# The exponent's argument in the mLSTM chunks: four operations with two sources and a per-partition scalar, one for each head, in place of a sum and a minimum over all heads

## The reference, cut to what matters

```python
D = bcum[..., :, None] - bcum[..., None, :] + ib[..., None, :]
D = jnp.where(mask, D, -jnp.inf)
g = bcum + m[..., None]
m_t = jnp.maximum(g, jnp.max(D, axis=-1))
inter = jnp.exp(g - m_t)
S = jnp.einsum('bhtd,bhsd->bhts', qb, kb) * jnp.exp(D - m_t[..., None])
num = jnp.einsum('bhts,bhsd->bhtd', S, vb) + inter[..., None] * jnp.einsum('bhvk,bhtk->bhtv', C, qb)
...
C_new = decay[..., None, None] * C + jnp.einsum('bhs,bhsv,bhsk->bhvk', w, vb, kb)
```

## Time and profile before

| What | us |
|---|---|
| median of 3 runs | 1199.9 |
| lowest and highest | 1199.41, 1201.68 |
| the profiled execution, own time | 1196.64 |
| its span, first to last instruction | 1194.9 |
| PE busy | 1144.2 (96%) |
| DVE busy | 706.8 (59%) |
| ACT busy | 428.1 (36%) |
| POOL busy | 305.2 (26%) |

### The profile page before, as it was taken

One profiled execution on the slowest core, in us unless ns is written; L12 is line 12 of the kernel. 1 busy time (PEld: TensorE's weight loads), 2 busy tenths in 40 slices (PEclk: granted clock), 3 DMA queues, 4 the chain that ended last, 5 costly groups with the idle time before them and its releaser, 6 DMA issues.

```text
span 1194.9 us, 19527 instructions
## 1 busy us (share of the span) xinstructions
PE 1144.2 (96%) x7381; PEld 1095.4 (92%) x7381; DVE 706.8 (59%) x1253; ACT 428.1 (36%) x716; POOL 305.2 (26%) x263
## 2 busy tenths in 40 slices
PE   5899999999989999999999999999999999999997
PEld 2698888888878999899999999999999999999996
DVE  4561455587876434787656655655645745656746
ACT  5552355545455343641320421321411311412331
POOL 0441101110535366771210210210210210210252
PEclk9999999999999999999999999999999999999998
DMA  8813334666343722120121121120120111111104
GB/s 305 312 62 111 108 107 141 202 191 203 105 135 118 245 72 71 37 71 27 45 71 36 37 71 36 53 70 18 53 70 18 70 53 31 56 53 36 36 1 142
DMA packets 61702, 109.87 MB, mean 92 GB/s; under 512 B 6434, under 2 KB 30278, under 8 KB 61254
## 3 DMA queue, kind: packets, MB, share of 16 engines
q1 hardware_dynamic: 51430, 84.88, 21.4%
q10 hardware_dynamic: 10208, 24.12, 6.5%
HBM read 96.81 MB, written 12.18 MB: 91 GB/s over the span
## 4 chain that ended last, share of the span: by engine, by line
PE 65%; DVE 3%; ACT 2%; issue 1%; POOL 0%; POOLq 0%; ACTq 0%; DVEq 0%
PE D L2297 13%; PE D L2299 13%; PE D L2298 13%; PE X L2299 5%; PE X L2297 5%; PE X L2298 5%; PE D L2113 3%; PE D L2115 3%; PE D L2114 3%; POOL H_lo L975 0%; DVE X L1556 0%; DVE B L1542 0%; ACT L1207 0%; DVE FU L1684 0%; DVE FU L1750 0%
## 5 line engine op out<-in xcount | busy, mean ns | idle before, releaser
L975 POOL TENSOR_TENSOR Y_lo<-FU,Y_hi 128x344 fp32r<-128x344 f32 (+2 forms) x120 | 123.1, 1030 | 555.3 <-ACT Y_hi L1115 548.9
L1831 DVE SCALAR_TENSOR_TENSOR X<-D,MOD,X 128x344 f32<-128x344 f32 (+1 forms) x216 | 123.8, 573 | 136.4 <-PE D L2299 113.9
L2297 PE MATMUL D<-Y_hi,W_hi 128*128 128x344 f32 x576 | 185.0, 321 | 0.0
L2298 PE MATMUL D<-Y_lo,W_hi 128*128 128x344 f32 x576 | 183.9, 319 | 0.0
L2299 PE MATMUL D<-Y_hi,W_lo 128*128 128x344 f32 x576 | 183.9, 319 | 0.0
L2113 PE MATMUL D<-H_hi,W_hi 128*128 128x344 f32 x472 | 157.7, 334 | 3.7 <-POOL H_lo L975 3.1
L2115 PE MATMUL D<-H_hi,W_lo 128*128 128x344 f32 x472 | 151.5, 321 | 0.0
L2114 PE MATMUL D<-H_lo,W_hi 128*128 128x344 f32 x472 | 151.5, 321 | 0.0
L2297 PEld LDWEIGHTS D<-Y_hi,W_hi 128*128 128x128 f32 x576 | 108.4, 188 | 1.2 <-issue 0.9
L2299 PEld LDWEIGHTS D<-Y_hi,W_lo 128*128 128x128 f32 x576 | 108.3, 188 | 0.0
L970 POOL TENSOR_TENSOR W_lo<-RAWW,W_hi 128x1024 fp32r<-128x1024 f32 x25 | 61.4, 2457 | 183.6 <-ACT W_hi L1110 183.1
(11 more groups left out here) (358 smaller groups left out, 2658.7 us busy)
## 6 DMA issues: line engine op xcount, KB each, us to landing
RAWW<-in_W SPq DMA_DIRECT2D x76, 512.0 KB, 3.6
RAWW<-in_WADA ACTq DMA_DIRECT2D x28, 512.0 KB, 4.3
RAWW<-in_WADA SPq DMA_DIRECT2D x20, 512.0 KB, 8.0
RAWW<-in_W ACTq DMA_DIRECT2D x18, 512.0 KB, 4.2
X0T<-in_x SPq DMA_DIRECT2D x3, 1376.0 KB, 12.6
out_y<-OUTN SPq DMA_DIRECT2D x24, 172.0 KB
X<-in_x SPq DMA_DIRECT2D x8, 344.0 KB, 4.4
NM<-nm_d SPq DMA_DIRECT2D x8, 256.0 KB, 6.0
```

Of the source, the lines that this page charges most:

```text
L975: nc.gpsimd.tensor_tensor(lo_v, fu_v, hi_v.bitcast(F32), ALU.subtract).then_inc(lo_ready, 1)
L1831: tell(V.scalar_tensor_tensor(out=tile(X, m_x, a, a + w), in0=DB[bank][:, 0:w], scalar=tile(MOD, m_g, 0, 1), in1=tile(X, m_x, a, a + w), o ...
L2297: T.matmul(out, w_h, hi(kt), start=(kt == 0), stop=False)
L2298: T.matmul(out, w_h, lo(kt), start=False, stop=False)
```

## The change

The two operations over 4 heads x 128 columns become four operations of 128 columns, each on one head: (`NM` + the head's column of `COL`) min `MASK`. Each of the first three is followed by a wait for itself (`link`), the last raises `ex_ready` as before. Nothing else is changed; the order of the steps is the same.

```diff
                     dve.wait_ge(ld_nm, 16 * (c + 1))
-                    link(V.tensor_tensor(EX[:], NM[:], wide(colh(0, c), LC), ALU.add))
-                    tell(V.tensor_tensor(EX[:], EX[:], over(MASK[:], HEADS), ALU.min), ex_ready, c + 1)
+                    for h in range(HEADS):
+                        one = V.scalar_tensor_tensor(out=EX[:, h, :], in0=NM[:, h, :], scalar=colh(0, c)[:, h:h + 1], in1=MASK[:],
+                                                     op0=ALU.add, op1=ALU.min)
+                        if h < HEADS - 1:
+                            link(one)
+                    tell(one, ex_ready, c + 1)
```

## The result

The change made the kernel **slower by 0.28%**: 1203.91 us median of 19 runs (1200.54 to 1206.23) against 1200.12 of 19 runs before (1196.86 to 1202.92), ratio 1.0028 with a 95% interval of 1.0020 to 1.0036, so 3.4 us with 2.4 to 4.3. The forecast was 1200.6, no measurable change, range 1198.6 to 1202.6. Two repeats gave 1.0013 (0.9998 to 1.0029) and 1.0019 (1.0008 to 1.0030). So the three series put the loss at 1.6 to 3.4 us; the interval of one of them still reaches no change.

What follows compares the result with a forecast made beforehand. PE was taken to lead the mixing stage, its waits mostly ending with DVE. Chunk delays of 0.09 + 0.27 + 0.3 = 0.7 us, put on the median 1199.9, gave 1200.6 us, range 1198.6 to 1202.6.

Steps and rivals of the forecast that it cites:

- The price of the added operations: DVE's `EX` step: 0.351 us per operation, 0.385 from start to start, 1.54 against 1.45 us, so 0.09 longer a chunk.
- The rival of the cheap operation: Each new DVE operation costs only 0.29 us, each step is 0.15 us shorter, 1199.15 us in all; chance 0.03.
- What of it reaches the end: Mixing stage, chunk by chunk: how much of DVE's longer step delays the end through PE's waits; 0.7 us in all.
- Chunks 0 to 4: Delay reaching the end: nothing in chunks 0 and 2, 0.09 (perhaps 0.2) us in 1, 0.09 each in 3 and 4.
- one of the two cases given: Chunk 1, L1722 before the change: POOL starts a little later, or one more short DVE instruction is left behind it.
- Chunk 6: POOL's L975 falls within the step, which ends at 328.7 to 328.85 instead of 328.50; 0.3 us reaches the end.
- Chunk 7: Taking turns with POOL, the step ends at about 363.5 instead of 362.25, hidden by ACT's table load; nothing reaches the end.
- Chunk 5: DVE is busy up to PE's wait, so 0.09 us reaches the end; L975 meets the step only in chunks 6 and 7.
- The rival on the slower side: POOL gets between the four operations: one L970 of 2.40 us in a step before PE's wait, 1203.0 us; chance 0.09.

Runs made afterwards that it cites:

- e4: The four operations in chunks 0 to 4 only, other chunks as in the kernel before: 1203.63 us, ratio 1.0015 to the kernel before.
- e3: The four operations in chunks 5 to 7 only, other chunks as in the kernel before: 1202.56 us, ratio 1.0007 to the kernel before.
- e6: The kernel before with extra matmuls, their results overwritten, in front of seven of PE's waits: 1198.49 us, ratio 0.9976 to the kernel before.
- e5: The changed kernel run again, nothing else altered: 1203.07 us, ratio 1.0013 to the kernel before.
- e7: The changed kernel with the same extra matmuls as e6: 1199.22 us, ratio 0.9988 to the kernel before.
- e13: The changed kernel without the three waits between its four operations, no extra matmuls: 1198.34 us, ratio 0.9995 to the kernel before.
- e15: The changed kernel run a third time, nothing else altered: 1201.60 us, ratio 1.0019 to the kernel before.
- e1: The kernel before run once more, unchanged, for the granted clock and span of its runs: 1201.08 us, ratio 0.9995.

## Why the prediction was wrong

- *The price of the added operations: right.* 0.351 us each, 0.385 from start to start, a step of 1.55 us against the 1.54 of the working. The rival of the cheap operation is out.
- *The failing step: "What of it reaches the end".* It gave 0.7 us; the runs gave 3.4 us in the first series and 1.6 and 2.3 in the repeats. For chunks 0 to 4 its terms add up to 0.27 us, and e4, the change in these chunks alone, measured 1.8 us (0.2 to 3.4). For chunks 5 to 7 they add up to 0.39 us, and e3 measured 0.8 (-0.5 to 2.3). The step added up delays between PE's waits and took PE's own speed as given. The one stretch at the lower clock stood in the earlier trace rows as 0.99, and I passed over it.
- *What the runs show in its place.* Pieces of the mixing stage at 1.2 GHz are longer by 1.3 to 2.6 us each in the profile of the changed kernel, 6.0 of the 6.2 us; at an equal clock the pieces grow by 0.2 us together, less than the 0.7. The kernel before has such stretches too: filling its waits gives 2.3 us (e6), and its own two profiles differ by as much as these two. Whether the change brings more of them is argued from e5 to e7 and not shown, so how the 3.4 us divide between the step's length, the clock and POOL stays open. What is shown is that the three waits are needed for the loss: without them it is gone (e13 against e15, 2.9 us).
- *Chunks 0 to 4: right in kind.* Chunk 0 was taken in by the loads, the waits behind chunks 1, 3 and 4 became 1.80, 1.58 and 0.78 us, where 1.60, 1.48 and 0.78 stood. L1725 was the one that met POOL's L970, as one of the two cases given.
- *Chunk 6: mis-sized.* 2.10 us to the next instruction, against 2.08 before, instead of 0.2 to 0.35 more. *Chunk 7:* 2.80 us from start to start in place of 2.06, expected 3.3, and covered by ACT's table as said: from its product to the output projection PE takes 27.22 us, before 27.28. *Chunk 5* met an L975, which the text excluded: POOL's L975 was 5.0 us later by then and the step only 3.4. In e15 both are 5.1 us later and don't meet.
- *The rival on the slower side named POOL and the wrong price.* No L970 fell into a step. Of the loss, the late chunks, where POOL takes turns with the four operations, hold 0.8 us (e3, -0.5 to 2.3).
- *The basis.* The one profile came from an execution 3.3 us under the median. I moved the sum to the median without asking what the other executions had that this one had not. In e1's it was the lower clock.

## What to carry to other kernels

Several small operations that write different parts of a tile needed no wait between them here: each wait costs more than the gap that the trace shows, here 0.12 us against 0.03, and three of them turned a shorter step into a longer one. Where PE waits for another engine by a microsecond and more, look at the granted clock of the stretch as well as at the wait, and compare several executions stage by stage before one is taken as the base. The mean clock over a launch isn't enough: it can be low where this costs nothing. If such a wait can't be removed, matmuls without use in its place can pay for themselves.

## What was not expected of the hardware

- Two operations of DVE without a wait between them overlap: 0.347 us long, 0.264 us from start to start; with a wait 0.385.
- Useless matmuls in front of seven waits made the launch 0.24% faster, the mean granted clock 0.994 in place of 0.988.
- The same program on the same chip had mean clocks from 0.978 to 0.996 in 35 runs, and its time ranged from 1197.65 to 1204.88 us. The fastest run of e13 has one of the two lowest means of its 11, 0.982, and most of its lower clock comes from the first 50 us of the launch.
